# Four norm boundaries of a transformer kernel, taken in token halves

## The chip, the cores and the metric

The kernel runs on one core of a Trainium2 chip. The metric is device time in microseconds (us), the median of several executions; less is better. The engines are TensorE (PE in the profile; PEld are its weight loads), VectorE (DVE), ScalarE (ACT), GpSimd (POOL) and the SP queue, which issues the weight transfers. Each runs its own instructions in order; they wait for one another by semaphores.

## The reference

Two layers on 512 tokens (256 context, 256 latent) of width 1024, in float32. Each layer is a half-step SwiGLU FFN, a token mixer (layer 0: gated DeltaNet beside differential attention; layer 1: retention) and another half-step FFN. Every sub-layer reads a normalised and modulated input and is added back through a gate:

```python
def ada_in(x, g, m, s):
    return rms_norm(x, g) * (1 + m[:, 3 * s + 1][:, None, :]) + m[:, 3 * s][:, None, :]
def swiglu(h, w_in, w_out):
    g, u = jnp.split(h @ w_in, 2, axis=-1)
    return (jax.nn.silu(g) * u) @ w_out
...
        x = x + 0.5 * ada_gate(m_lat, 0) * swiglu(ada_in(x, norm_w[l, 0], m_lat, 0), ffn_w_in[l, 0], ffn_w_out[l, 0])
```

`rms_norm` divides each token by the root of its mean square over the 1024 features. Context tokens use their own modulation vector. The last norm is plain.

## The kernel before

**Layout.** `x` is held transposed: 8 chunks (`KD`) of 128 features on the partitions, 512 tokens along a row, context in columns 0 to 255 (`CTX`), latent in 256 to 511 (`LAT`). A float32 product is made of three products in `F32R`: weights and activations are each split in a hi and a lo part, and lo x hi, hi x lo and hi x hi are added in PSUM. Products on 512 columns are lines 812 to 814 (up and mixer steps, `products`) and 883 to 885 (`pe_down`). Where only latent tokens are live, `joint_products` (824, 825) runs w_hi on 512 columns, the hi and lo halves together, and w_lo on 256.

**Steps.** All weights go through one list of steps, `runs`. A step has a weight tile of up to 128x2048: SP loads `w_raw` (377), ScalarE copies it to `w_hi` (`split_hi`, 432), VectorE makes `w_lo` (`split_lo`, 586). There are two slots. The hi part of step s waits until step s-2's products are done, the load of step s until step s-2's lo part is made. TensorE starts step s when its lo part is there and its accumulator is free (`pe_ready`). Each engine's walk over a run of steps (`walk`) takes the first `skip` steps straight, then pairs in a hardware loop, then the rest.

**FFN.** The up steps make a gate and a value column block (16 x 3 products a step), ScalarE applies Silu (444; for latent alone a Copy at 441 and a Silu at 449), VectorE multiplies (620; 609 and 614), and the product is split (451, 625). The down steps (8 chunks, 12 or 10 blocks each, so 36 or 30 products) end in `x += gate * product` (653, two operations, one per stream). VectorE also works off `ada_tile`s (595), which make the modulation vectors from weights that GpSimd loads.

**A norm boundary.** While a down run whose sums are wanted goes on, ScalarE squares each new chunk of x (479) and VectorE adds the squares (644). After the last chunk, TensorE sums over partitions by products with ones (859), ScalarE takes the root (501), VectorE the reciprocal (699), TensorE broadcasts it to all partitions (899). Then, per chunk of 512 tokens, VectorE normalises (713), ScalarE scales and shifts, one operation per stream (513), ScalarE copies the hi part (518) and VectorE subtracts for the lo part (717). TensorE takes the first step of the next stage as the lo parts arrive. Seven norms: `n00` at the start, `n01` between the first FFN and the mixer (stage `diff`), `n02` after the mixer's output (`about`, 24 products a chunk) before `up1a`, `n10` before `up2a`, `n11` before retention (`retq`, latent columns alone, `joint_products`), `n12` and `fin`.

The order at a boundary is written out by hand, for VectorE as

```python
        dve_down(dve, "down0b", "n00", BOTH, 2, norm="n01")
        dve_mod(dve, "n01")
        dve_inverse(dve, "n01", 0)
        dve_modulate(dve, "n01")
        dve_left_tile(dve)
        dve_ab(dve)
```

In the retention queries ScalarE copies a step's result (1955), VectorE adds to it (2043), and TensorE rotates it (1885) after the next step's products.

Of the kernel before, what the change touches and what calls it, by code (L numbers as in the profile page):

```python
# [18 lines left out]
F32 = mybir.dt.float32  # L19
# [6 lines left out]
P = 128  # L26
D = 1024
# [98 lines left out]
def build(nc, a):  # L126
# [162 lines left out]
    def walk(eng, name, body, tallies=(), skip=0):  # L289
# [3 lines left out]
        looped = (n - 2 - skip) // 2  # L293
# [46 lines left out]
    chunks_before = {n: KD * i for i, n in enumerate(norms)}  # L340
# [93 lines left out]
    def act_up(act, name, cols):  # L434
# [18 lines left out]
        walk(act, name, body)  # L453
# [7 lines left out]
    def adds_before(norm):  # L461


        return 1 + (KD - 2) * (norms.index(norm) - 1)

    def sums_before(norm):

        return 0 if norm == "n00" else KD + norms.index(norm) - 1
# [15 lines left out]

    def act_down_norm(act, name, norm, cols):
        s0 = R[name][1]

        def body(s, slot, r, ahead):
            if isinstance(r, int) and r == KD - 1:

                act.activation(warm_root[:], vecs[:, 2:3], ACT.Sqrt).then_inc(warmed, 1)
# [4 lines left out]
        walk(act, name, body, skip=2)  # L496

# [37 lines left out]
    def scalar_program(act):  # L535
# [16 lines left out]
        act_root(act, "n01", 0, 1.0 / D)  # L552
        act_modulate(act, "n01")
        act_ab(act)
        act_down_norm(act, "about", "n02", ALL)
        act_root(act, "n02", 0, 1.0 / D)
        act_modulate(act, "n02")
# [4 lines left out]
        act_root(act, "n10", 0, 1.0 / D)  # L562
        act_modulate(act, "n10")
# [4 lines left out]
        act_root(act, "n11", 0, 1.0 / D)  # L568
        act_modulate(act, "n11")
# [63 lines left out]
    def dve_down(dve, name, norm_gate, streams, ada, norm=None):  # L633
# [6 lines left out]
        def body(s, slot, r, ahead):  # L640
            if norm and not (isinstance(r, int) and r < 2):
                dve.wait_ge(sq_ready, chunks_before[norm] + r)
# [3 lines left out]
            dve.wait_ge(step_done, s + 1)  # L646
# [12 lines left out]
            if ada and not (ada == 2 and isinstance(r, int) and r == KD - 1):  # L659
# [4 lines left out]
    def dve_left_tile(dve):  # L664
        ada_tile(dve, ada_next[0] - 1, (ada_next[0] - 1) % 2)
# [31 lines left out]
    def dve_inverse(dve, norm, t0):  # L697
        dve.wait_ge(root_done, norms.index(norm) + 1)
        dve.reciprocal(norm_columns(norm, t0, 8), norm_columns(norm, t0, 0)).then_inc(inverse_done, 1)

    def dve_modulate(dve, norm):

        base_c, cols = chunks_before[norm], streams_of(norm)
        dve.wait_ge(rstd_done, norms.index(norm) + 1)
# [28 lines left out]
    def vector_program(dve):  # L733
# [23 lines left out]
        dve_up(dve, "up0b", ALL, 2)  # L757
        dve_down(dve, "down0b", "n00", BOTH, 2, norm="n01")
        dve_mod(dve, "n01")
        dve_inverse(dve, "n01", 0)  # L760
        dve_modulate(dve, "n01")
        dve_left_tile(dve)
        dve_ab(dve)
        dve_gate(dve, "n01")
        dve_down(dve, "about", "n01", BOTH, 0, norm="n02")
        dve_mod(dve, "n02")
        dve_inverse(dve, "n02", 0)
        dve_modulate(dve, "n02")
# [1430 lines left out]
```

## Time and profile before

| | |
|---|---|
| median of three runs | 2210.33 us (2209.47 to 2213.39) |
| profiled execution | 2210.68 us, span 2209.0 us |
| TensorE busy | 2060.1 us, 93% of the span |
| VectorE busy | 1309.5 us, 59% |
| ScalarE busy | 794.9 us, 36% |
| mean granted TensorE clock | 0.966 |

Products are pipelined: a product's own time in the profile contains its way through the array, and what it costs in a row is the distance from one start to the next. The granted clock is 1.00 at 2.4 GHz and 0.50 at 1.2 GHz.

### The profile page before, as it was taken

How to read it: one execution, taken by the hardware profiler on the slowest of the kernel's cores; microseconds unless marked ns; L12 is line 12 of the kernel's file. 1: busy time of each engine (PE TensorE's matmuls, PEld its weight loads, DVE VectorE, ACT ScalarE, POOL GpSimd, SP SyncE). 2: the span in 40 equal slices, each digit the busy share in tenths (PEclk: the TensorE clock that was granted, in tenths of full speed). 3: DMA queues.
4: the chain of work that ended last, by engine and by line, in shares of the span. 5: the costliest groups of instructions: out<-in, count | busy, mean ns of one | idle time of the engine just before them, and what ended most of it. 6: DMA issues, size and time to landing. Idle time of an engine off the chain costs nothing.

```text
span 2209.0 us, 27575 instructions
## 1 busy us (share of the span) xinstructions
PE 2060.1 (93%) x9882; PEld 1721.1 (78%) x9882; DVE 1309.5 (59%) x1801; ACT 794.9 (36%) x1001; POOL 112.9 (5%) x173
## 2 busy tenths in 40 slices
PE   6999999897898978899999989999989999898998
PEld 6788888785587877788888878888877788677887
DVE  4677578746544675577677753363345524765666
ACT  2432222323444232532122253212234225846543
POOL 1000000000000230000000000000000000100000
PEclk9999999898898998999999999999998999999999
DMA  8355555521020000355555622343232223123453
GB/s 310 111 193 180 177 183 174 185 77 58 2 91 31 1 1 29 116 193 181 185 172 184 196 95 95 98 160 127 73 124 94 78 96 135 56 98 139 168 193 126
DMA packets 53989, 275.37 MB, mean 125 GB/s; under 512 B 6928, under 2 KB 8208, under 8 KB 36496
## 3 DMA queue, kind: packets, MB, share of 16 engines
q1 hardware_dynamic: 34032, 200.86, 26.5%
q0 software_dynamic: 19728, 72.88, 10.4%
q8 instruction: 58, 0.95, 0.2%
q10 hardware_dynamic: 144, 0.46, 0.1%
q14 instruction: 27, 0.22, 0.0%
HBM read 273.13 MB, written 1.05 MB: 124 GB/s over the span
## 4 chain that ended last, share of the span: by engine, by line
PE 81%; DVE 7%; ACT 6%; issue 4%; DMA 1%; ACTq 0%; DVEq 0%; POOL 0%; SPq 0%
PE ps L812 15%; PE ps L814 15%; PE ps L813 15%; PE ps L824 7%; PE ps L883 6%; PE ps L885 6%; PE ps L884 6%; PE ps L825 3%; ACT w_hi L432 1%; PE ps L921 1%; ACT sil L513 1%; DVE w_lo L586 1%; PE ps L1511 1%; PE ps L859 1%; PE ps L1507 1%
## 5 line engine op out<-in xcount | busy, mean ns | idle before, releaser
L812 PE MATMUL ps<-h_parts,w_lo 128*128 128x512 f32 x1480 | 585.5, 396 | 15.2 <-DVE h_parts L717 14.8
L813 PE MATMUL ps<-h_parts,w_hi 128*128 128x512 f32 x1480 | 580.8, 392 | 0.0
L814 PE MATMUL ps<-h_parts,w_hi 128*128 128x512 f32 x1480 | 580.4, 392 | 0.0
L432 ACT ACTIVATE w_hi<-w_raw 128x2048 fp32r<-128x2048 f32 (+3 forms) x207 | 354.0, 1710 | 532.7 <-PE ps L885 292.4
L586 DVE TENSOR_TENSOR w_lo<-w_raw,w_hi 128x2048 fp32r<-128x2048 f32 (+3 forms) x207 | 421.9, 2038 | 145.2 <-ACT w_hi L432 144.5
L595 DVE SCALAR_TENSOR_TENSOR ada_product<-ada_w,silu_c 128x1024 bf16<-128x1024 f32 x272 | 332.7, 1223 | 44.6 <-DMA ada_w<-in_ada 14.2
L812 PEld LDWEIGHTS ps<-h_parts,w_lo 128*128 128x128 f32 x1480 | 281.1, 190 | 78.1 <-issue 16.7
L813 PEld LDWEIGHTS ps<-h_parts,w_hi 128*128 128x128 f32 x1480 | 281.0, 190 | 59.4 <-issue 1.4
L814 PEld LDWEIGHTS ps<-h_parts,w_hi 128*128 128x128 f32 x1480 | 280.8, 190 | 59.4
L444 ACT ACTIVATE sil<-ps 128x512 f32<-128x512 f32 x66 | 39.5, 598 | 495.6 <-PE ps L814 495.6
L824 PE MATMUL ps<-h_parts,w_hi 128*128 128x512 f32 x544 | 200.4, 411 | 11.6 <-DVE h_parts L717 7.5
L883 PE MATMUL ps<-hid_parts,w_lo 128*128 128x512 f32 x528 | 205.4, 389 | 0.0
L884 PE MATMUL ps<-hid_parts,w_hi 128*128 128x512 f32 x528 | 205.4, 389 | 0.0
L885 PE MATMUL ps<-hid_parts,w_hi 128*128 128x512 f32 x528 | 205.4, 389 | 0.0
L620 DVE TENSOR_TENSOR prod<-sil,ps 128x512 f32<-128x512 f32 x66 | 45.4, 688 | 192.1 <-ACT sil L444 192.1
L825 PE MATMUL ps<-h_parts,w_lo 128*128 128x256 f32 x544 | 154.9, 285 | 0.0
L653 DVE SCALAR_TENSOR_TENSOR x<-ps,mod,x 128x256 f32 (+1 forms) x160 | 72.3, 481 | 132.0 <-PE ps L885 107.8
L824 PEld LDWEIGHTS ps<-h_parts,w_hi 128*128 128x128 f32 x544 | 104.6, 192 | 43.4 <-issue 6.9
L408 POOL DMA_DIRECT2D ada_w<-in_ada x136 | 72.0, 529 | 1038.5 <-DVE ada_product L595 1032.7
L884 PEld LDWEIGHTS ps<-hid_parts,w_hi 128*128 128x128 f32 x528 | 99.1, 188 | 20.7
L885 PEld LDWEIGHTS ps<-hid_parts,w_hi 128*128 128x128 f32 x528 | 99.1, 188 | 20.6
L883 PEld LDWEIGHTS ps<-hid_parts,w_lo 128*128 128x128 f32 x528 | 99.1, 188 | 20.5
(275 smaller groups left out, 2143.5 us busy)
## 6 DMA issues: line engine op xcount, KB each, us to landing
w_raw<-in_w_up SPq DMA_DIRECT2D x88, 1024.0 KB, 4.9
ada_w<-in_ada POOLq DMA_DIRECT2D x136, 512.0 KB, 3.8
w_raw<-in_w_down SPq DMA_DIRECT2D x32, 768.0 KB, 4.2
w_raw<-in_w_ret SPq DMA_DIRECT2D x24, 1024.0 KB, 4.9
w_raw<-in_w_down SPq DMA_DIRECT2D x32, 640.0 KB, 3.9
w_raw<-in_w_ab SPq DMA_DIRECT2D x14, 1024.0 KB, 4.9
w_raw<-in_w_ret_out SPq DMA_DIRECT2D x8, 1024.0 KB, 4.9
ada<-in_ada SPq DMA_DIRECT2D x8, 512.0 KB, 19.7
```

What stands on the lines that cost most here:

```text
L432: act.activation(w_hi[slot][:, 0:elems], w_raw[slot][:, 0:elems], ACT.Copy).then_inc(hi_ready, 1)
L586: dve.tensor_tensor(w_lo[slot][:, 0:elems], w_raw[slot][:, 0:elems], w_hi[slot][:, 0:elems].bitcast(F32), ALU.subtract).then_inc(lo_ready, 1)
L595: dve.scalar_tensor_tensor(out=ada_product[:], in0=ada_w[:, slot, :], scalar=1.0, in1=silu_c[:, st, :], op0=ALU.mult, op1=ALU.mult, accum_ ...
L653: last = dve.scalar_tensor_tensor(out=xc, in0=ps[:, 2 * slot, cols], scalar=mod[:, k, 2, st, bass.ds(r, 1)], in1=xc, op0=ALU.mult, op1=ALU ...
L812: pe.matmul(out, lo, rhs_hi(k), start=first and k == 0, stop=False)
L813: pe.matmul(out, hi, rhs_lo(k), start=False, stop=False)
L814: mm = pe.matmul(out, hi, rhs_hi(k), start=False, stop=last and k == nk - 1)
L824: pe.matmul(out, w_hi[slot][:, off:off + P], parts, start=start, stop=stop, skip_group_check=True)
L825: return pe.matmul(out[:, LAT], w_lo[slot][:, off:off + P], parts[:, 1], start=False, stop=stop, skip_group_check=True)
L883: pe.matmul(ps[:, 2 * slot, cols], wlo, hi, start=k == 0, stop=False)
L884: pe.matmul(ps[:, 2 * slot, cols], whi, lo, start=False, stop=False)
L885: mm = pe.matmul(ps[:, 2 * slot, cols], whi, hi, start=False, stop=k == nk - 1)
```

## The change

At `n01`, `n02`, `n10` and `n11` (`SEAMS`) the last two chunks of the down run and the first two steps of the next stage are taken in two halves of the tokens. The first half is CTX at the first three and LAT at `n11`.

- TensorE (`tail` in `pe_down`): chunk 6 and chunk 7 for the first half, each 3 x `nk` products of 256 columns; the first column sums of that half; chunk 6 for the second half, with the last two sums after its fourth block; the broadcasts of the first half; chunk 7 for the second half. Then `pe_seam_pairs`: step 0 and step 1 on the first half, then both on the second. Sums and broadcasts of the second half stand after the first, third and eighth block of step 0. At `n11`, `seam_queries` takes the two query steps whole (they have latent columns alone), with the same sums in between.
- VectorE (`dve_seam`): x updates by half. The modulation is three operations per chunk and half: VectorE `x * scale * broadcast`, ScalarE hi part `= scaled + shift`, VectorE lo part `= (scaled + shift) - hi`. Four scaled parts fit in `prod` and `sil`.
- The splits for the next stage's two steps stand inside this: the first before the first lo part, the second after the last lo part of the first half.
- `dve_mod` moves ahead of the down run. Two ada tiles instead of one are left for after the boundary (`n01`, `n10`).
- At `n11` ScalarE's first query copy and the first `retk` step wait for all lo parts.
- ScalarE's walk over the latent up runs (`up3a`, `up3b`) is straight code instead of a loop.

```diff
-    def walk(eng, name, body, tallies=(), skip=0):
+    def walk(eng, name, body, tallies=(), skip=0, unrolled=False):
...
-        looped = (n - 2 - skip) // 2
+        looped = 0 if unrolled else (n - 2 - skip) // 2
...
+    TAIL = KD - 2
+    SEAMS = {"n01": (CTX, LAT), "n02": (CTX, LAT), "n10": (CTX, LAT), "n11": (LAT, CTX)}
...
-        walk(act, name, body)
+        walk(act, name, body, unrolled=cols == LAT)
...
+    def act_seam(act, norm, s6):
...
+        act.activation(warm_root[:], vecs[:, 2:3], ACT.Sqrt).then_inc(warmed, 1)
+        for i in range(2):
+            act.wait_ge(sq_added, adds_before(norm) + TAIL - 2 + i)
+            square(0, i)
+        root(0)
+        split_hi(act, s6 + 2, s6 % 2, ELEMS[s6 + 2])
+        for c in range(4):
+            shift(0, c)
+        square(1, 0)
+        shift(0, 4)
+        shift(0, 5)
+        square(1, 1)
+        shift(0, 6)
+        shift(0, 7)
+        split_hi(act, s6 + 3, (s6 + 1) % 2, ELEMS[s6 + 3])
+        root(1)
+        for c in range(KD):
+            shift(1, c)
...
+    def dve_seam(dve, norm, gate, s6):
...
+        for i in range(2):
+            dve.wait_ge(seam_made, seam_count(norm, 0, 1) + i + 1)
+            place(0, i)
+        dve.wait_ge(mod_ready, k + 1)
+        inverse(0)
+        scale(0, 0)
+        scale(0, 1)
+        dve.wait_ge(step_done, s6 + 1)
+        place(1, 0)
+        scale(0, 2)
+        scale(0, 3)
+        split_lo(dve, s6 + 2, s6 % 2, ELEMS[s6 + 2])
+        for c in range(4):
+            low(0, c)
+            scale(0, c + 4)
+            if c == 0:
+                dve.wait_ge(step_done, s6 + 2)
+                place(1, 1)
+        for c in range(4, KD):
+            low(0, c)
+        split_lo(dve, s6 + 3, (s6 + 1) % 2, ELEMS[s6 + 3])
+        inverse(1)
...
+    def pe_seam_pairs(pe, name, norm, s6):
+        s0 = R[name][1]
+        for half, cols in enumerate(SEAMS[norm]):
+            for r in range(2):
+                slot = (s0 + r) % 2
+                if half == 0:
+                    pe_ready(pe, s0 + r)
+                for k in range(KD):
+                    if r == 0:
+                        pe.wait_ge(seam_lo, seam_count(norm, half, KD) + k + 1)
+                    for u in range(2):
+                        mm = products(pe, ps[:, 2 * slot + u, cols], slot, u * D + k * P, 1, lambda _: h_hi[:, k, cols],
+                                      lambda _: h_lo[:, k, cols], k == 0, k == KD - 1)
+                    if half == 0:
+                        pe_seam_second(pe, norm, s6, KD * r + k)
...
+        def tail(pe):
+            s6 = s0 + TAIL
+            for i in range(2):
+                pe_ready(pe, s6 + i)
+                half_chunk(i, 0).then_inc(seam_made, 1)
+            pe_seam_sum(pe, norm, 0, s6, 0)
...
+            half_chunk(0, 1, first).then_inc(step_done, 1)
+            pe_seam_spread(pe, norm, 0)
+            half_chunk(1, 1).then_inc(step_done, 1)
...
+            if r == 0:
+                act.wait_ge(seam_lo, seam_count("n11", 2, KD))
```

## Rows read from the trace of the kernel before

**Rows 1.** The page: busy time

```profile
PE 2060.1 (93%) x9882; PEld 1721.1 (78%) x9882; DVE 1309.5 (59%) x1801; ACT 794.9 (36%) x1001; POOL 112.9 (5%) x173
```

**Rows 2.** Stretches around the four boundaries; busy time by engine, granted clock

```profile
413.08:462.37 49.29, 43.36 (x181) 35.33 (x180) 31.41 (x45) 23.70 (x34) 1.58 (x3) 0.86 0.39 133
890.60:936.68 46.08, 39.30 (x169) 32.13 (x168) 29.29 (x44) 24.48 (x36) 0.60 (x1) 0.89 0.31 108
1260.36:1309.46 49.10, 42.58 (x182) 34.23 (x180) 31.76 (x48) 26.09 (x37) 1.58 (x3) 0.90 0.39 134
1633.14:1676.77 43.63, 35.35 (x151) 27.60 (x150) 23.77 (x33) 24.53 (x36) 0.00 (x0) 0.80 0.23 79
```

**Rows 3.** The same view of the hole between down run and mixer

```profile
426.68:437.53 10.85, 5.16 (x26) 4.56 (x25) 6.45 (x14) 5.40 (x9) 0.53 (x1) 0.61 0.61 225
```

**Rows 4.** Timeline of the first boundary

```profile
413.08 0.39 PE L883 MATMUL ps<-hid_parts,w_lo 128*128 128x512 f32 x1
...
426.45 0.39 PE L885 MATMUL ps<-hid_parts,w_hi 128*128 128x512 f32 x1
...
429.42 1.87 PE L859 MATMUL ps<-const,prod 128*128 128x1 f32 x8 [0.92 <-ACT prod L479]
...
431.92 2.07 PE L899 MATMUL ps<-const,small 128*128 128x128 f32 x8 [0.64 <-DVE small L699]
...
437.53 0.76 PE L812 MATMUL ps<-h_parts,w_lo 128*128 128x512 f32 x1 [3.53 <-DVE h_parts L717]
```

**Rows 5.** The stretch after that hole

```profile
437.53:442.65 5.12, 5.12 (x12) 4.05 (x13) 3.54 (x6) 4.72 (x9) 0.00 (x0) 0.50 0.00 0
```

**Rows 6.** Groups of instructions by form; mean ns of one

```profile
L586 DVE TENSOR_TENSOR w_lo<-w_raw,w_hi 128x2048 fp32r<-128x2048 f32 x134 | 306.9, 2291 | 119.8 <-ACT w_hi L432 119.7
L812 PEld LDWEIGHTS ps<-h_parts,w_lo 128*128 128x128 f32 x1480 | 281.1, 190 | 78.1 <-issue 16.7 <-DVE h_parts L717 2.9 <-ACT df_o L1095 0.7
...
L432 ACT ACTIVATE w_hi<-w_raw 128x2048 fp32r<-128x2048 f32 x134 | 256.1, 1911 | 260.9 <-PE ps L814 153.5 <-PE ps L885 68.7 <-PE ps L825 26.3
...
L513 ACT ACTIVATE sil<-prod,mod 128x256 f32<-128x256 f32 x88 | 48.3, 591 | 37.9 <-DVE prod L713 37.4
...
L653 DVE SCALAR_TENSOR_TENSOR x<-ps,mod,x 128x256 f32 x96 | 43.3, 481 | 88.0 <-PE ps L885 73.8 <-PE ps L825 13.3 <-DVE mod L689 0.4
...
L614 DVE TENSOR_TENSOR prod<-sil 128x256 f32<-128x256 f32 x22 | 9.2, 418 | 0.0
...
L451 ACT ACTIVATE hid_parts<-prod 128x256 f32 x18 | 7.5, 418 | 37.8 <-DVE prod L614 37.8
...
L449 ACT ACT_TABLE_LOAD x5 | 6.4, 1283 | 0.1
```

**Rows 7.** Timeline of one latent up step with table load

```profile
2040.69 0.50 PE L824 MATMUL ps<-h_parts,w_hi 128*128 128x512 f32 x1 [1.06 <-DVE w_lo L586]
```

**Rows 8.** Stretches in the two latent up runs and one wait in the queries

```profile
2014.46:2075.10 60.64, 57.21 (x322) 48.83 (x321) 37.19 (x41) 41.51 (x50) 0.00 (x0) 1.00 0.47 165
2121.74:2161.29 39.55, 39.55 (x226) 34.27 (x225) 26.11 (x29) 21.84 (x28) 0.00 (x0) 1.00 0.51 176
...
1690.20:1691.40 1.20, 0.00 (x0) 0.00 (x0) 0.69 (x1) 1.20 (x2) 0.00 (x0) 1.00 1.00 423
```

**Rows 9.** Timeline of latent products, 512 and 256 columns in turn

```profile
2100.00 0.40 PE L824 MATMUL ps<-hid_parts,w_hi 128*128 128x512 f32 x1
...
2100.23 0.28 PE L825 MATMUL ps<-hid_parts,w_lo 128*128 128x256 f32 x1
...
2100.35 0.39 PE L824 MATMUL ps<-hid_parts,w_hi 128*128 128x512 f32 x1
```

**Rows 10.** Timeline of VectorE ahead of the third boundary

```profile
1260.79 0.88 DVE L653 SCALAR_TENSOR_TENSOR x<-ps,mod,x 128x256 f32 x2 [1.03 <-PE ps L885]
...
1263.29 1.22 DVE L595 SCALAR_TENSOR_TENSOR ada_product<-ada_w,silu_c 128x1024 bf16<-128x1024 f32 x1
...
1264.67 1.23 DVE L595 SCALAR_TENSOR_TENSOR ada_product<-ada_w,silu_c 128x1024 bf16<-128x1024 f32 x1 [0.16 <-DVE ada_product L595]
```

More of the change, by code:

```diff
@@ L339, in build, with seam_count, stream, token_tiles @@
     norms = ["n00", "n01", "n02", "n10", "n11", "n12", "fin"]
-    chunks_before = {n: KD * i for i, n in enumerate(norms)}
+    TAIL = KD - 2
+    SEAMS = {"n01": (CTX, LAT), "n02": (CTX, LAT), "n10": (CTX, LAT), "n11": (LAT, CTX)}
+    whole = [n for n in norms if n not in SEAMS]
+    chunks_before = {n: KD * i for i, n in enumerate(whole)}
+    seam_before = {n: i for i, n in enumerate(SEAMS)}
+    squares_before, count = {}, 0
+    for n in norms:
+        squares_before[n] = count
+        count += TAIL if n in SEAMS else KD
+    seam_made, seam_placed, seam_squared = sem("seam_made"), sem("seam_placed"), sem("seam_squared")
+    seam_summed, seam_rooted, seam_inverse, seam_spread = (sem(f"seam_{n}") for n in ("summed", "rooted", "inverse", "spread"))
+    seam_scaled, seam_hi, seam_lo = sem("seam_scaled"), sem("seam_hi"), sem("seam_lo")
+    def seam_count(norm, half, per):
+        return (2 * seam_before[norm] + half) * per
+    def stream(cols):
+        return 0 if cols == CTX else 1
+    def token_tiles(cols):
+        return range(cols.start // P, cols.stop // P)
     ups_before = {}
@@ L496, in act_down_norm, with scaled_part, square, root @@
         walk(act, name, body, skip=2)
+    def scaled_part(c, cols):
+        return (prod[:, 0, cols], prod[:, 1, cols], sil[:, 1, cols], sil[:, 0, cols])[c % 4]
+    def act_seam(act, norm, s6):
+        k = norms.index(norm)
+        done = seam_count(norm, 0, 1)
+        def square(half, i):
+            cols = SEAMS[norm][half]
+            if half == 0:
+                act.wait_ge(seam_placed, done + i + 1)
+            else:
+                act.wait_ge(acc_free, s6 + i + 3)
+            act.activation(prod[:, (s6 + i) % 2, cols], x[:, TAIL + i, cols], ACT.Square).then_inc(seam_squared, 1)
+        def root(half):
+            t = token_tiles(SEAMS[norm][half])
+            act.wait_ge(seam_summed, done + half + 1)
+            act.activation(norm_columns(norm, 0, 0)[:, t.start:t.stop], ps[:, SEAM[half], t.start:t.stop], ACT.Sqrt,
+                           bias=vecs[:, 2:3], scale=1.0 / D).then_inc(seam_rooted, 1)
+        def shift(half, c):
+            cols = SEAMS[norm][half]
+            act.wait_ge(seam_scaled, seam_count(norm, half, KD) + c + 1)
+            act.activation(h_hi[:, c, cols], scaled_part(c, cols), ACT.Identity,
+                           bias=mod[:, k, 1, stream(cols), c:c + 1]).then_inc(seam_hi, 1)
+        act.activation(warm_root[:], vecs[:, 2:3], ACT.Sqrt).then_inc(warmed, 1)
[16 more added lines that the diff above has]
+            shift(1, c)
     def act_root(act, norm, t0, scale):
@@ L658, in body @@
                 split_lo(dve, s + 2, slot, ahead)
-            if ada and not (ada == 2 and isinstance(r, int) and r == KD - 1):
+            if ada:
                 ada_tile(dve, t0 + r, (t0 + slot + R[name][1]) % 2)
@@ L861, in pe_ssq, with pe_seam_sum @@
         return mm
+    def pe_seam_sum(pe, norm, half, s6, part):
+        cols, bank = SEAMS[norm][half], SEAM[half]
+        if part == 0:
+            pe.wait_ge(sq_added, adds_before(norm) + TAIL - 1)
+        pe.wait_ge(seam_squared, 4 * seam_before[norm] + 2 * half + part + 1)
+        operands = (sil[:, 0], prod[:, s6 % 2]) if part == 0 else (prod[:, (s6 + 1) % 2],)
+        for n, squares in enumerate(operands):
+            for t in token_tiles(cols):
+                mm = pe.matmul(ps[:, bank, t:t + 1], squares[:, t * P:(t + 1) * P], ones[:, 0:1],
+                               start=part == 0 and n == 0 and t == cols.start // P, stop=part == 1, skip_group_check=True)
+        if part == 1:
+            mm.then_inc(seam_summed, 1)
```

170 lines of the change are left out of this document (129 added, 41 removed).

## The prediction

> **What bounds the kernel now.** Start with the page. TensorE is busy 93% of the span [rows 1], so time can only be saved where TensorE stands or runs slowly. The stretches around the four boundaries show where. I take each from the first product of the second-last down chunk (t = 0 below) to the first product of the third step after the boundary: 49.29, 46.08, 49.10 and 43.63 us, at a mean granted clock of 0.80 to 0.90 [rows 2]. At the first, 10.85 us lie between the last down product and the first product of the next stage [rows 3]. The timeline shows what fills them: 1.0 us of waiting and the column sums (429.42), the broadcasts (431.92), then TensorE waits 3.53 us more for VectorE's first lo part and starts at 437.53 [rows 4]. ScalarE's and VectorE's splits for the next two steps run in the same hole. The clock falls in it and stays at 0.50 for the first twelve products, which take 5.12 us [rows 5], 0.427 each; sixty before the hole, the first at 413.08 and the last at 426.45 [rows 4], are 0.227 apart, so the low clock costs 12 x 0.2 = 2.4 us. Over the whole stretch this boundary loses 49.3 - 156 x 0.227 = 13.9 us (sixty down products, 96 of two steps); the second loses 46.1 - 144 x 0.227 = 13.4 and the third 13.7.
>
> A second place is the last up loop. In the first of its two runs table loads of 1.28 us stand between ScalarE's copy and Silu (five are recorded at 449) [rows 6], the split is late by them, and TensorE waits for lo weights, 1.06 us at 2040.69 [rows 7]. Ten such steps take 60.64 us, while seven steps without loads take 39.55 us, 5.65 us each [rows 8].
>
> **Prices.** A 256-column product: 2100.23 to 2100.35, 0.117 us, with its own weights and with the next ones loaded meanwhile; a 512-column one takes 0.23 beside it [rows 9]. This is the number on which the change hangs, because it makes 1032 half products (456 in the chunk pairs, 576 in the steps) out of 516 whole ones: 1032 x 0.117 - 516 x 0.227 = 3.6 us. Lower bound: half of 0.227, which is nothing extra. Upper bound: the 0.19 us that one weight load is shown with [rows 6], which would be 79 us extra. I take 0.117, since that row is the very form.
>
> VectorE, 256 columns: 0.481 us with PSUM, 0.418 without; two in a row take 0.88 [rows 10], so 0.40 apart. I take 0.44 for a scale or an x update and 0.46 for a lo part, which the next scale waits for. ScalarE: 0.418 plain, 0.591 with scale and bias [rows 6]; the new shift has a bias only, I take 0.50 with the handover. Splits: 1.91 and 2.29 us for 2048 elements [rows 6], the latter 2.25 when work follows. Column sums and broadcasts: eight take 1.87 and 2.07 us at the low clock [rows 4], 0.23 and 0.26 each; bounds are that and half of it, and I take half, 0.11, as the clock should be high.
>
> The Trainium skill speaks against half products: "TensorE: Matmul & The Clock Gate", What overlaps and what doesn't, says that a weight load overlaps running products only when its row group differs. All loads here use all rows. With that page's formula the load is about 107 ns, so the half products would come to some 0.213 us and the change would be about 99 us dearer than by the row, as an estimate. The row does not agree: 768 columns and two loads take 0.35 us together [rows 9].
>
> **First boundary, step by step** (us after t = 0). Half chunks of 30 products take 3.5. TensorE: 3.5, 7.0 (both chunks, first half), four sums 7.45, twelve products 8.85, two sums 9.1, eighteen 11.2, two broadcasts 11.4, last half chunk 14.9. The first needs of this are met: the second chunk's lo weights are there at 2.9 as before (VectorE goes on from that split at 1263.29, t being 1260.36) [rows 10]; x update, square and add for the first half end near 8.2, before the second sums; root and reciprocal near 9.9, before the broadcasts. An ada tile of 2.6 us (two operations 1.38 apart [rows 10]) stands ahead of the first x update on VectorE and still leaves it at 6.3.
>
> From the broadcasts on VectorE is the path: handover 0.16, four scales and an x update 2.2, split of the next step's weights 2.25 (its hi part, asked for at 11.4, is done by 13.3), lo part 0.46, handover 0.15: 5.2. First product 16.6, so TensorE stands 1.7. VectorE then offers a lo part every 0.92, the second after 1.38 (another x update), while TensorE needs 0.70; the fourth scale of the second four ends 3.7 after the first lo part. ScalarE's shift (0.55) and split of the following weights (1.96), VectorE's split (2.25), reciprocal (0.2) and the broadcasts (0.4) follow: second step's first half starts 8.9 after the first, at 25.5. In it TensorE has 5.6 + 0.7 of work, so 2.6 stay empty. From there on nothing is missing: first half 5.6, two second halves 11.2; VectorE finishes the second half's lo parts at 32.4, the first is wanted at 31. End 42.3 against 49.3: **7.0 saved**.
>
> The third step's weights must be ready by then. Step one now ends at 36.7 only, 5.6 before step two. ScalarE's split 38.9; VectorE has two left ada tiles instead of one: four operations 1.38 apart [rows 10], 5.4, from 32.4 to 37.8; copy of step one 1.22 (the width of the tile's operation), split 2.25: 41.5 with the handovers. Covered by 0.8; without that cover the surplus is paid one for one. The SP queue's load of the third step waits for the first split (16.1) and has 20 us. Moving the modulation vectors ahead of the down loop (three operations on 16 columns) costs nothing: all its ada tiles precede it, and VectorE stands 1 us per chunk there [rows 10].
>
> **Other boundaries.** The third is the same: 49.1 - 42.3 = **6.8**; after it the gate and the up product take the copy's place, still under 42.3. The second has chunks of 24 products: broadcasts end at 9.3, first product 14.5, end 40.2: 46.1 - 40.2 = **5.9**; TensorE stands 2.4 there first, as only 2.8 of the 5.2 is covered. At the fourth only the chunks are halved; the two query steps take latent columns and run whole. Here the change adds a wait: ScalarE's copy of the first query step waits for all sixteen lo parts (32.4), since it overwrites scaled parts. Behind it stand its split and, on TensorE, the rotation. Copy and split to 34.9, VectorE's split 37.2: third step at 37.4 where it was 43.6, **6.2**. TensorE is through with step two at 31 and stands 6.
>
> **Up loop.** Ten steps at 5.65 are 56.5 for 60.64: **4.1**, if no load is left; the second up loop of this stage shows the same instructions without one [rows 8]. "ScalarE: Activation LUTs", Table sets, in the Trainium skill has copy in every set; that fits.
>
> Sum 7.0 + 5.9 + 6.8 + 6.2 + 4.1 = 30.0. The profiled execution took 2210.68 (span 2209.0), 0.35 above the median of 2210.33: **2180.3 us**. Most of each hole is not removed, it is cut into two pauses with work between.
>
> **Rivals.** (1) *The pauses are longer and the clock falls in them.* Fourteen VectorE operations and four handovers stand on the path: 0.05 to 0.1 more each is 1 us a boundary. For a fall: a mean of 0.61 over the 10.85 us at the first boundary [rows 3] means that it came after (0.61 - 0.5) / 0.5 x 10.85 = 2.4 us, with sums running. Against: a wait of 1.3 us at 1690 passed at 1.00 [rows 8]. A fall costs up to 2.4; 3.4 x 4 = 13.6 less: 2194. The 1.7 us of slack in the second pause hides part. (2) *Half products are bound by their weight loads.* The slower side: 1032 x (0.19 - 0.117) = 75, so 2180 + 75 = 2255. It turns the sign when a half product takes 0.117 + 30/1032 = 0.146. Against it stands the form's own row. (The page on TensorE named above states a rule of this kind.) (3) *The boundary does not shrink*: the same splits and 256-column operations with twice the fixed part refill the hole; only the up loop's 4.1 stays, 2206. For it: the new path holds two VectorE splits and one of ScalarE, 6.5 us, where the old hole held one of each, 4.2. Against: 3.5 us of down products and 5.6 of the first step now lie beside it. (4) *More gain*: VectorE at 0.40 throughout and no third pause at the queries, 2172.
>
> **Chances.** Forecast 0.55, (1) 0.23, (2) 0.07, (3) 0.06, (4) 0.06, something slower that I do not see 0.03. Around 2180 the unknown prices (0.40 to 0.48 on VectorE, 0.42 to 0.59 on ScalarE) move it by 5 either way. The range that leaves out no more than two in ten reaches from 2172 to 2198. Of a measurement here 0.2%, 4.4 us, can be told from nothing. Faster by more: the forecast, (1), (4) and 0.01 of (3), 0.85; within: the rest of (3), 0.05; slower: 0.10.
>
> **What would show it.** Half products spaced 0.117 to 0.12; pauses of about 1.7 and 2.6 us (2.4 and 2.6 at the second, one of 6 in the queries) in place of 10.7; granted clock 1.00 from t = 0 to 42; the ada tiles after the second lo parts, with no TensorE wait behind them; no table loads in the last up steps. Wrong if the spacing is 0.15 or more, if VectorE's chain from broadcast to lo part is over 7 us, or if the third step waits for its split.

## The result and the profile after

The changed kernel takes 2190.44 us in the median of six runs (2185.98 to 2194.33), the kernel before 2210.68 beside it: ratio 0.991, 95% interval 0.9897 to 0.9922. That is 20 us less, inside the range (2172 to 2198); 30 less were forecast. The profiled execution took 2188.84 us (span 2187.2), 21.8 less than the one of before. The page's first line, to be held against [rows 1]:

```profile
PE 2058.6 (94%) x10430; PEld 1748.2 (80%) x10430; DVE 1319.4 (60%) x1865; ACT 761.3 (35%) x972; POOL 112.9 (5%) x173
```

The four boundaries, cut at the same two products as in [rows 2]; after start, end and length come the busy time of TensorE's products, its weight loads, VectorE, ScalarE and GpSimd, then the granted clock, the DMA share and GB/s:

```profile
413.24:457.32 44.08, 42.84 (x345) 42.58 (x344) 33.52 (x58) 18.15 (x29) 1.58 (x3) 0.96 0.36 126
884.16:927.51 43.35, 41.39 (x322) 41.22 (x320) 26.72 (x50) 19.05 (x31) 0.00 (x0) 0.92 0.24 88
1251.22:1294.97 43.75, 41.51 (x345) 41.12 (x344) 33.93 (x61) 20.56 (x32) 1.58 (x3) 1.00 0.37 125
1618.68:1657.19 38.51, 32.28 (x220) 29.26 (x218) 25.99 (x47) 21.04 (x32) 0.00 (x0) 0.92 0.26 89
```

They save 5.2, 2.7, 5.35 and 5.1 us, 18.4 together, where 7.0, 5.9, 6.8 and 6.2 were forecast, 25.9. TensorE's timeline at the first boundary, and the second pause at the third:

```profile
413.24 0.28 PE L1060 MATMUL ps<-hid_parts,w_lo 128*128 128x256 f32 x1
413.36 0.28 PE L1061 MATMUL ps<-hid_parts,w_hi 128*128 128x256 f32 x1
...
420.50 0.58 PE L1010 MATMUL ps<-const,sil 128*128 128x1 f32 x4
420.94 0.58 PE L1010 MATMUL ps<-const,prod 128*128 128x1 f32 x4
421.38 0.36 PE L1060 MATMUL ps<-hid_parts,w_lo 128*128 128x256 f32 x1
...
425.50 0.60 PE L1019 MATMUL ps<-const,small 128*128 128x128 f32 x4
425.86 0.36 PE L1060 MATMUL ps<-hid_parts,w_lo 128*128 128x256 f32 x1
...
429.41 0.28 PE L1062 MATMUL ps<-hid_parts,w_hi 128*128 128x256 f32 x1
430.93 0.35 PE L947 MATMUL ps<-h_parts,w_lo 128*128 128x256 f32 x1 [1.24 <-DVE h_parts L776]
...
439.61 0.60 PE L1019 MATMUL ps<-const,small 128*128 128x128 f32 x4
...
1275.88 0.28 PE L949 MATMUL ps<-h_parts,w_hi 128*128 128x256 f32 x1
1277.15 0.71 PE L1019 MATMUL ps<-const,small 128*128 128x128 f32 x4 [1.00 <-DVE small L756]
```

Pauses are given here from the start of one product to the start of the next; 0.12 of that is the spacing that two products always have. The hole of 10.85 us [rows 3] is now one pause of 1.52 at the first boundary, ahead of the first product of the next stage, and two at the third, 1.52 and 1.27. At the first boundary the second pause is missing in this trace: TensorE ran at the low clock before it and was late itself. From the first half product to the end of chunk 7's last are 16.3 us where 14.9 were forecast. At the second boundary the first pause is longer and the clock falls behind it:

```profile
897.31 0.28 PE L1062 MATMUL ps<-h_parts,w_hi 128*128 128x256 f32 x1
899.55 0.35 PE L947 MATMUL ps<-h_parts,w_lo 128*128 128x256 f32 x1 [1.96 <-DVE h_parts L776]
```

The stretches at the low clock behind the first pause of the first two boundaries, with the busy times of the instructions on `h_parts` alone (no GpSimd column):

```profile
432.80:436.20 3.40, 2.89 (x14) 2.67 (x14) 2.35 (x6) 1.37 (x3) 0.50 0.58 243
900.40:907.20 6.80, 4.96 (x22) 4.71 (x22) 2.93 (x7) 1.59 (x4) 0.50 0.36 143
```

VectorE and ScalarE behind the first broadcasts of the first boundary:

```profile
425.75 1.92 ACT L456 ACTIVATE w_hi<-w_raw 128x2048 fp32r<-128x2048 f32 x1 [2.05 <-PE ps L1062]
...
428.10 2.29 DVE L654 TENSOR_TENSOR w_lo<-w_raw,w_hi 128x2048 fp32r<-128x2048 f32 x1
430.31 0.48 DVE L776 SCALAR_TENSOR_TENSOR h_parts<-prod,mod,h_parts 128x256 fp32r<-128x256 f32 x1
...
434.88 1.90 ACT L456 ACTIVATE w_hi<-w_raw 128x2048 fp32r<-128x2048 f32 x1
436.68 0.24 ACT L546 ACTIVATE small<-ps,vecs 128x2 f32<-128x2 f32 x1
...
436.81 2.29 DVE L654 TENSOR_TENSOR w_lo<-w_raw,w_hi 128x2048 fp32r<-128x2048 f32 x1 [0.79 <-ACT w_hi L456]
439.02 0.16 DVE L756 RECIPROCAL small<-small 128x2 f32<-128x2 f32 x1
```

Ten steps of the first latent up run (60.64 in [rows 8]):

```profile
1995.10:2051.65 56.55, 56.55 (x322) 49.05 (x321) 37.43 (x40) 32.62 (x43) 0.00 (x0) 1.00 0.47 164
```

At the Copy and the Silu of these steps the kernel before has ten table loads recorded, five at each line (441 and 449); the changed one has one, in both runs together. The third steps behind the first three boundaries start without a wait, as forecast.

The whole account of the two profiled executions: boundaries 18.4 less, first up run 4.1 less, second 1.0 less, the mixer behind the first boundary 1.4 less; the retention stage, from the third step after the fourth boundary to the last norm's sums, is 3.3 longer (320.0 against 316.7). That makes 21.6 of 21.8.

### The profile page after: what moved, and what is told of

Read it like the earlier page. It is cut to its first block, busy times and chain, and to the rows that moved or that the text cites. A ratio compares the mean times of both kernels' runs of the same rounds, so it can differ in the third digit from the quotient of the medians.

```text
span 2187.2 us, 28339 instructions
## 1 busy us (share of the span) xinstructions
PE 2058.6 (94%) x10430; PEld 1748.2 (80%) x10430; DVE 1319.4 (60%) x1865; ACT 761.3 (35%) x972; POOL 112.9 (5%) x173
## 4 chain that ended last, share of the span: by engine, by line
PE 85%; DVE 7%; ACT 4%; issue 2%; DMA 1%; POOL 0%; SPq 0%; ACTq 0%; DVEq 0%
PE ps L947 15%; PE ps L948 15%; PE ps L949 15%; PE ps L959 8%; PE ps L1100 5%; PE ps L1101 5%; PE ps L1102 5%; PE ps L960 4%; PE ps L1138 1%; DVE w_lo L654 1%; ACT w_hi L456 1%; PE ps L1724 1%; PE ps L1720 1%; DMA const<-in_const 1%; PE ps L1060 1%
## 5 line engine op out<-in xcount | busy, mean ns | idle before, releaser
L947 PE MATMUL ps<-h_parts,w_lo 128*128 128x512 f32 (+1 forms) x1576 | 601.2, 381 | 8.4 <-DVE h_parts L776 4.4
L948 PE MATMUL ps<-h_parts,w_hi 128*128 128x512 f32 (+1 forms) x1576 | 596.7, 379 | 0.0
L949 PE MATMUL ps<-h_parts,w_hi 128*128 128x512 f32 (+1 forms) x1576 | 596.3, 378 | 0.0
L947 PEld LDWEIGHTS ps<-h_parts,w_lo 128*128 128x128 f32 x1576 | 299.8, 190 | 65.1 <-issue 5.3
L948 PEld LDWEIGHTS ps<-h_parts,w_hi 128*128 128x128 f32 x1576 | 299.6, 190 | 55.4 <-issue 1.4
L949 PEld LDWEIGHTS ps<-h_parts,w_hi 128*128 128x128 f32 x1576 | 299.5, 190 | 54.5
L959 PE MATMUL ps<-h_parts,w_hi 128*128 128x512 f32 x544 | 198.1, 407 | 6.3 <-DVE h_parts L860 2.5
L1100 PE MATMUL ps<-hid_parts,w_lo 128*128 128x512 f32 x468 | 182.1, 389 | 0.0
L1101 PE MATMUL ps<-hid_parts,w_hi 128*128 128x512 f32 x468 | 182.1, 389 | 0.0
L1102 PE MATMUL ps<-hid_parts,w_hi 128*128 128x512 f32 x468 | 182.1, 389 | 0.0
L726 DVE SCALAR_TENSOR_TENSOR x<-ps,mod,x 128x256 f32 (+1 forms) x144 | 65.3, 481 | 121.1 <-PE ps L1102 96.9
L959 PEld LDWEIGHTS ps<-h_parts,w_hi 128*128 128x128 f32 x544 | 105.1, 193 | 33.9 <-DVE w_lo L654 5.0
L960 PEld LDWEIGHTS ps<-h_parts,w_lo 128*128 128x128 f32 x544 | 105.7, 194 | 0.2 <-issue 0.2
L1100 PEld LDWEIGHTS ps<-hid_parts,w_lo 128*128 128x128 f32 x468 | 87.8, 188 | 18.4
L1101 PEld LDWEIGHTS ps<-hid_parts,w_hi 128*128 128x128 f32 x468 | 87.8, 188 | 18.2
```

The lines of the kernel that those rows point to most:

```text
L947: pe.matmul(out, lo, rhs_hi(k), start=first and k == 0, stop=False)
L948: pe.matmul(out, hi, rhs_lo(k), start=False, stop=False)
L949: mm = pe.matmul(out, hi, rhs_hi(k), start=False, stop=last and k == nk - 1)
L959: pe.matmul(out, w_hi[slot][:, off:off + P], parts, start=start, stop=stop, skip_group_check=True)
L960: return pe.matmul(out[:, LAT], w_lo[slot][:, off:off + P], parts[:, 1], start=False, stop=stop, skip_group_check=True)
L1100: pe.matmul(ps[:, 2 * slot, cols], wlo, hi, start=k == 0, stop=False)
```

## The experiments

Each was run beside the kernel before; differences between kernels of one group are the better guide, since the same changed kernel gave 0.991 and 0.9896.

**The parts apart.** First the halves without the new order (`halves_only`): as many half products, in the old sequence.

```diff
+    def halved_pairs(pe, s, slot, norm=None):
+        for part in (CTX, LAT):
+            for k in range(KD):
+                ...
+                for u in range(2):
+                    mm = products(pe, ps[:, 2 * slot + u, part], slot, u * D + k * P, 1, ...)
```

> The kernel before with nothing changed but the width of products: the last two chunks of the four down runs and the first two steps after three of the boundaries (not after the fourth) are taken as 256-column products, all of the context half, then all of the latent half. No order between engines changes. 1032 half products in place of 516 whole ones, 96 x 3 = 288 of them in first steps that wait for lo parts anyway. Theory A (a product has a fixed part of about 0.014 us beside its columns, as 0.227 - 512 / 2400 columns per ns shows): half products are 0.1205 apart as in the changed kernel, so + 7.3 us at most, + 5 to 7 expected, 2216. Theory B (the row of the latent products, 0.117): + 3.6 at most, 2213. Rival C (bound by weight loads, 0.19): + 50 or more.

2235.46 us, ratio 1.0124 (1.0105 to 1.0143): slower by 26 us. The spacing settles what was asked: 120 half products stand 0.120 apart, which makes 7 us of the 26 (1032 x 0.120 against 516 x 0.227).

```profile
427.19 0.28 PE L894 MATMUL ps<-hid_parts,w_lo 128*128 128x256 f32 x1
427.31 0.28 PE L895 MATMUL ps<-hid_parts,w_hi 128*128 128x256 f32 x1
427.44 0.28 PE L896 MATMUL ps<-hid_parts,w_hi 128*128 128x256 f32 x1
```

The rest I had overlooked. The old modulation still takes both halves at once and gives a lo part only every 1.3 to 1.9 us. The first half of step 0 is paced by it to the end, and all of the second half comes behind:

```profile
437.56 0.69 DVE L717 TENSOR_TENSOR h_parts<-sil,h_parts 128x512 f32 x1 [1.37 <-ACT h_parts L518]
...
450.12 0.69 DVE L717 TENSOR_TENSOR h_parts<-sil,h_parts 128x512 fp32r<-128x512 f32 x1 [1.19 <-ACT h_parts L518]
```

This boundary took 55.80 us (413.16 to 468.96) for 49.29, at about the mean clock of before (0.88 for 0.86). The second took 53.60 for 46.08 and the third 57.39 for 49.10, and there the clock has a share as well: at the second it stayed at 0.50 for 20 us (before, 10), and the mean fell from 0.89 to 0.81:

```profile
894.99:948.59 53.60, 46.00 (x313) 43.59 (x312) 29.30 (x44) 24.47 (x36) 0.92 (x2) 0.81 0.28 100
```

No run parts the pacing from the clock. Halving alone costs; here it paid only together with a new order around it.

Then the straight loop alone (`unroll_only`):

```diff
-        looped = (n - 2 - skip) // 2
+        looped = 0 if unrolled else (n - 2 - skip) // 2
```

> The kernel before with ScalarE's latent up runs as straight code and nothing else. The prediction's term is 4.1 us, 2206.6. By the traces the change gave 4.1 in the first of the two runs (ten steps 60.6 to 56.5) and 1.0 in the second (nine steps 50.9 to 49.9), so 5.1, 2205.6, if both come from the straight code. If the second run's 1.0 comes from something else, 2206.6.

2205.68 us, ratio 0.9989 (0.9979 to 0.9998), 3.7 less, with an interval that reaches from 0.4 to 4.6. The trace is the better guide: the ten steps take 56.52 us for 60.64, 4.1 less.

```profile
2009.70:2066.22 56.52, 56.52 (x322) 48.98 (x321) 37.40 (x40) 32.60 (x42) 0.00 (x0) 1.00 0.48 164
```

And the boundaries without the straight loop (`seams_only`):

```diff
-        walk(act, name, body, unrolled=cols == LAT)
+        walk(act, name, body)
```

> The changed kernel with ScalarE's latent up runs in a loop again; the boundaries stay in halves. If the terms add up it gives 20.2 - 5.1 = 15 us against the kernel before, 2195.5; the four stretches around the boundaries measured 18.4 together in the two traces, the rest of the mixers' stages takes some back. A rival, that part of what the boundaries seem to give is only shifted into the later stages, would show as less than 12.

2193.55 us, ratio 0.9936 (0.9917 to 0.9956), 15.9 less. 15.9 and 3.7 add up to 19.6, within noise of the 20.2 measured together, and the shortfall lies in the part with the boundaries (25.9 forecast).

**The two pauses.** Four kernels in one group. First the changed kernel once more (`after_again`):

> The changed kernel itself, once more, as the measure for the three kernels beside it. Its first six runs spread over 8 us, so its place against the kernel before is taken again: 2190 us, ratio 0.991.

2187.9 us, 0.9896 (0.988 to 0.9912). Its first boundary took 43.81 with the clock at 1.00 where it took 44.08 with a fall: there a fall costs only 0.3, because the second pause (1.27) takes it up. The four together took 169.5 us, for 169.7.

Then `early_split`: ScalarE rounds the following weights before its fifth shift (not the first, as the expectation has it), and VectorE takes the reciprocal before it splits them.

```diff
         square(1, 0)
+        split_hi(act, s6 + 3, (s6 + 1) % 2, ELEMS[s6 + 3])
         shift(0, 4)
...
-        split_lo(dve, s6 + 3, (s6 + 1) % 2, ELEMS[s6 + 3])
         inverse(1)
+        split_lo(dve, s6 + 3, (s6 + 1) % 2, ELEMS[s6 + 3])
```

> At the first boundary of the changed kernel ScalarE makes the first half's shifted chunks before it rounds the next weights (w_hi, 1.9 us), and VectorE splits those weights (2.3 us) before it takes the reciprocal for the second half. Here the rounding stands ahead of the first shift and the split behind the reciprocal. Theory 1, the second pause ends with VectorE's chain reciprocal, scale, place, so what stands in front of it counts: the pause at the second half shrinks by 0.8 to 1.1 us in each boundary, 3 to 4 us in all, 2186 to 2187 us. Theory 2, the weights split is what the second half's last products wait for or the first pause grows by the rounding's 1.9 us as the shifts come later: no gain or up to 4 us slower. The pause ahead of the first product after the half chunks tells them apart: 1.5 us stays (theory 1) or grows (theory 2).

2184.56 us, 0.9878 (0.9861 to 0.9895). The runs of the two kernels overlap in time; in the trace the second pause is gone, and the boundaries take 42.55, 43.33, 42.49 and 36.94 us, 4.4 less than the first trace of the changed kernel and 4.1 less than the second. 1.3 of it is the first boundary and 1.3 the third, both at a clock of 1.00 before and after. Theory 1; the first pause stayed 1.52.

```profile
436.12 0.16 DVE L756 RECIPROCAL small<-small 128x2 f32<-128x2 f32 x1
436.19 2.27 DVE L654 TENSOR_TENSOR w_lo<-w_raw,w_hi 128x2048 fp32r<-128x2048 f32 x1
```

```profile
438.15 0.28 PE L949 MATMUL ps<-h_parts,w_hi 128*128 128x256 f32 x1
438.27 0.60 PE L1019 MATMUL ps<-const,small 128*128 128x128 f32 x4
```

Then `filled`, the changed kernel with products in its pauses that nobody reads:

```diff
+    def fill(pe, count):
+        for _ in range(count):
+            pe.matmul(ps[:, 7, 0:SEQ], ident, const[:, C_COSD:C_COSD + SEQ], start=True, stop=True)
...
+            fill(pe, 5)
...
+            fill(pe, 6 if nk == FB else 9)
```

The five stand ahead of the second half's broadcasts, the six or nine behind the last half chunk.

> The changed kernel with TensorE products that nobody reads put into its two pauses at each boundary (6 or 9 of 256 columns in fp32 behind the last half chunk, 5 ahead of the second half's broadcasts). It computes the same. Theory 1, the pauses cost twice, once as idle time and once by the clock of 1.2 GHz that follows them (3.4 us after the first pause at the first boundary, 6.8 us at the second): with the pauses filled the granted clock stays at 1.00 in the boundaries, and the time falls by 1.7 us at the second boundary and 0.3 to 0.6 at the others, 2 to 3 us in all, 2187 to 2188 us. Theory 2, the clock falls for what went before the pauses (the spaced sums and broadcasts) and not for them: the clock falls as before, and the time stays or grows by what the fillers take beyond the pauses, up to 1 us for each boundary.

2193.73 us, 0.9928 (0.9914 to 0.9943): slower than the changed kernel, and still theory 1 on the clock. It stayed at 1.00 through the first three boundaries, of which two are shown:

```profile
413.28:459.11 45.83, 45.83 (x368) 45.17 (x366) 33.51 (x58) 18.15 (x29) 1.58 (x3) 1.00 0.35 122
887.34:931.43 44.09, 44.09 (x349) 43.36 (x348) 26.71 (x50) 18.94 (x31) 0.00 (x0) 1.00 0.24 86
```

But I had sized a filler at 0.24 us. In fp32 the trace records each as two rows, 0.216 apart, so six take 2.6 us in a pause of 1.5 and hold up the product behind them:

```profile
429.56 2.75 PE L1044 MATMUL ps<-const 128*128 128x256 f32 x12
431.97 0.47 PE L947 MATMUL ps<-h_parts,w_lo 128*128 128x256 f32 x1
```

`both` has the edits of early_split and of filled.

> The two edits together. If both theories 1 hold and don't overlap: 5 to 7 us below the changed kernel, 2183 to 2185 us. If the shorter second pause already keeps the clock up, the gains don't add: 3 to 5 us.

2198.14 us, 0.9948 (0.9934 to 0.9962). Neither expectation: with five fillers in the second pause the fillers are what the broadcasts wait for, and moving the split can't help (first boundary 45.83 again).

**What sets the first pause.** Three kernels on top of early_split. `split_first`:

```diff
         place(1, 0)
+        split_lo(dve, s6 + 2, s6 % 2, ELEMS[s6 + 2])
         scale(0, 2)
         scale(0, 3)
-        split_lo(dve, s6 + 2, s6 % 2, ELEMS[s6 + 2])
```

> early_split, and VectorE splits the next weights (2.29 us) straight behind the placing, before the third and fourth scaling and not after them. Theory 1, the first pause is the ring of weights: the slot comes free with the first whole-chunk half (425.4 us at the first boundary), then ScalarE's rounding 1.92, VectorE's split 2.29 and one low operation 0.48 follow, against 4.0 us of half products, so the split's start counts, and it was held by two scalings until 428.10 where the rounding had ended at 427.67: the pause falls from 1.52 to 1.1 us (from 2.24 to 1.8 at the second boundary), 0.4 each, 1.6 us in all below early_split. Theory 2, VectorE's whole queue up to the last low operation sets the pace and not the split's place in it: the 0.4 us come back as small waits between the first half's products, and the time equals early_split's.

2191.16 us, 0.9915 (0.9901 to 0.9928). Both theories missed: the pause grew, from 1.52 to 1.90.

```profile
427.74 2.29 DVE L654 TENSOR_TENSOR w_lo<-w_raw,w_hi 128x2048 fp32r<-128x2048 f32 x1 [0.30 <-ACT w_hi L456]
429.94 0.87 DVE L769 SCALAR_TENSOR_TENSOR sil<-x,mod,ps 128x256 f32<-128x256 f32 x2
430.73 0.48 DVE L776 SCALAR_TENSOR_TENSOR h_parts<-prod,mod,h_parts 128x256 fp32r<-128x256 f32 x1
```

The two scalings still stand ahead of the first lo part, and VectorE now idles 0.30 for ScalarE's rounding. The first product waits for the sum of VectorE's queue, not for the split's place in it. The four boundaries together took 3.8 us more than in early_split (169.1 for 165.3), and the ratio is 0.0037 higher, 8 us; the longer pause is 1.5 of that, the rest is not explained.

`split_parts`:

```diff
+        def split_part(n):
+            ...
+            part = [w[s6 % 2][:, 0:2 * D].rearrange("p (u d) -> p u d", u=2)[:, :, n * D // 2:(n + 1) * D // 2]
+                    for w in (w_lo, w_raw, w_hi)]
+            dve.tensor_tensor(part[0], part[1], part[2].bitcast(F32), ALU.subtract) \
+               .then_inc(lo_ready if n else seam_split, 1)
```

> early_split, and the split of the next weights in two operations, chunks 0 to 3 before the first low operation and chunks 4 to 7 before the fourth; TensorE waits for the second at its fifth chunk. Theory 1 (the ring of weights): the pause falls by half a split, 1.1 us, to 0.4 us (1.1 at the second boundary), and the fifth chunk may wait 0.5 us: 2.5 to 4.4 us below early_split. Theory 2 (VectorE's whole queue sets the pace): the fifth chunk waits for all that the pause gave back, and the time equals early_split's.

2187.92 us, 0.9893 (0.9878 to 0.9908). Theory 2 at the first boundary: the pause fell to 0.45, the fourth chunk then came 0.81 behind the sums ahead of it and the fifth 0.31 behind the fourth, and the boundary took 42.54 for 42.55. The second took 40.73 for 43.33: its pause was 1.17 for 2.24, and the low clock behind it lasted 3.4 us for 6.8, so that this gain is in good part the clock's. At the fourth boundary, whose products are written out apart and wait for the whole split, my edit made them wait for its later second half, 4.2 us:

```profile
1633.65 0.28 PE L1078 MATMUL ps<-hid_parts,w_hi 128*128 128x256 f32 x1
1637.88 0.80 PE L970 MATMUL ps<-h_parts,w_hi 128*128 128x512 f32 x1 [3.95 <-DVE w_lo L786]
```

The fillers once more, shorter and in the first pause only (`fit`; the diff is against both):

```diff
-            fill(pe, 5)
...
-            fill(pe, 6 if nk == FB else 9)
+            fill(pe, 3 if nk == FB else 4)
```

> early_split with unread fp32 products only in the first pause, and by the length that the filled kernel showed of one (two rows of 0.216 us): 3 of them, 1.3 us in a pause of 1.52, and 4, 1.7 us in 2.24 at the second boundary. In the filled kernel the granted clock stayed at 1.00 in the first three boundaries, but its fillers were longer than the pauses and held the path. Theory 1, the clock falls for the pause: it stays at 1.00 at the second boundary, whose 43.33 us become 41.6 to 42, and nothing else is late; 1.5 to 3 us below early_split. Theory 2, what the rest of the pause leaves idle is enough to let the clock fall: as early_split.

2183.65 us, 0.9881 (0.9865 to 0.9897): as early_split in the median (which had 0.9878). So the times don't tell the theories apart. In the trace the second boundary is where theory 1 has it, and below: 40.26 for 43.33, at 1.00, with the first at 42.55 as in early_split.

```profile
413.50:456.05 42.55, 42.55 (x351) 42.05 (x350) 33.40 (x58) 18.16 (x29) 1.58 (x3) 1.00 0.40 132
883.36:923.62 40.26, 40.03 (x330) 39.50 (x329) 26.61 (x50) 18.92 (x31) 0.00 (x0) 1.00 0.26 95
```

Last, the split in two operations again, at the first three boundaries only, with fillers where a pause stays (`parts_fit`; the diff is against split_parts and fit):

```diff
         for c in range(4):
-            if c == 3:
-                split_part(1)
             low(0, c)
+            if c == 3 and norm != "n11":
+                split_part(1)
             scale(0, c + 4)
...
-            fill(pe, 3 if nk == FB else 4)
+            fill(pe, {"n02": 2, "n11": 3}.get(norm, 0))
```

> fit, with the split in two operations at the first three boundaries only (the fourth has its products written out elsewhere, where TensorE still waits for the whole split), and its second operation behind the fourth low operation and not ahead of it. The fillers stay where a pause of over 1 us stays: 2 at the second boundary, 3 at the fourth. Theory 1, the place of the split counts: the pause is 0.45 us, and the fifth chunk, which split_parts served 1.0 us late, is served 0.4 to 0.5 us late, so the boundaries take 42.0 us (42.55 in fit) and 39.8 (40.26): 1.5 us in all below fit, ratio 0.9875. Theory 2, VectorE's queue up to the last low operation sets the pace: the boundaries take what they took in fit, within 0.1 us. That would be too little for the medians, so the boundaries' own times in the trace decide.

2178.39 us (2177.78 to 2183.63), ratio 0.9859 (0.9842 to 0.9875): the fastest here, 32 us below the kernel before, though its profiled execution, the slowest of its runs, has a span of 2182.0 where fit's has 2179.9. The boundaries took 42.39, 40.12, 42.34 and 36.96 us, 0.15 less than in fit at each of the first three: nearer theory 2. That is 0.5 us in all four for 5 in the medians, and the intervals of the two ratios overlap (fit's is 0.9865 to 0.9897), so this pair doesn't show that parts_fit is the faster. The first pause gave 1.07 back, the fifth chunk took 0.78:

```profile
433.96 0.28 PE L963 MATMUL ps<-h_parts,w_hi 128*128 128x256 f32 x1
434.87 0.35 PE L961 MATMUL ps<-h_parts,w_lo 128*128 128x256 f32 x1 [0.62 <-DVE h_parts L777]
```

**The floor under smaller products.** `quarter` cuts the half products of the two last down chunks once more:

```diff
-                pe.matmul(ps[:, 2 * slot + half, cols], wlo, hi, start=k == 0, stop=False)
+                for t in range(2):
+                    pe.matmul(ps[:, 2 * slot + half, tile], wlo, hi[:, q], start=k == 0, stop=False, ...)
```

> The changed kernel with each half product of the two last down chunks cut once more, into two of 128 columns with the same weights loaded for each (240 for 120 at a boundary of ten chunks, 192 for 96 at the second). It computes the same. Theory 1, a product costs its columns and a fixed 0.014 us (512 columns 0.227, 256 columns 0.120): 0.067 us apart, 1.6 us more for each boundary, 6 us in all. Theory 2, the load of 128 rows of weights is a floor that 256 columns only just cover: the column sums, a weight load each with one column, stand 0.084 to 0.110 apart, and the quarter products do too: 6 to 12 us more for each boundary, 22 to 45 in all.

One run, 2285.83 us. Against the expectation, the sums of these two chunks aren't the reference's; why was not tested. Only the times are read.

```profile
413.29 0.28 PE L1063 MATMUL ps<-hid_parts,w_hi 128*128 128x128 f32 x1
413.40 0.28 PE L1064 MATMUL ps<-hid_parts,w_hi 128*128 128x128 f32 x1
413.52 0.28 PE L1062 MATMUL ps<-hid_parts,w_lo 128*128 128x128 f32 x1
```

```profile
413.23:428.30 15.07, 15.07 (x137) 15.06 (x135) 6.31 (x10) 4.11 (x6) 0.53 (x1) 1.00 0.43 154
428.30:453.90 25.60, 25.60 (x123) 25.60 (x122) 5.29 (x9) 4.59 (x8) 0.00 (x0) 0.50 0.11 42
```

Theory 2: 120 such products stand 0.111 apart, hardly closer than half products of twice the columns at 0.120. 912 of them in place of 456 are 46 us, theory 2's upper figure; the time is 95 us above the changed kernel's, for a reason in neither theory: the granted clock fell to 0.50 although TensorE was never idle (15.07 busy of 15.07), and stayed there for 34 us. By the mean clocks of the two traces (0.947 and 0.971) some 115 us more ran at the low level, which is worth up to 57 us, as an estimate.

## Why the prediction was right, and where it was off

**Half products.** Right in kind, a little mis-sized: 0.120 apart and not 0.117. Over 1032 products that is 3.1 us more, 6.7 in all for halving. 0.117 was read from one pair whose neighbour was a 512-column product; for halves among themselves the longer row is the price. Rival 2 (0.19 us each) is excluded. Its bound was a recorded duration; quarter shows that products with a load each can stand 0.111 apart while each load is still recorded with 0.19. By the rule in the Trainium skill, "TensorE: Matmul & The Clock Gate", What overlaps and what doesn't, the halves would have stood near 0.213, as the prediction estimated; the measurement decides against it. The same page of the Trainium skill, LDWEIGHTS, gives the time of a load as its columns divided by 1.2 ns, an estimate of 107 ns for 128; the 0.111 of quarter agrees with that.

**Column sums and broadcasts.** The largest term that was mis-sized, and by a misreading. The eight of [rows 4] that take 1.87 us are four instructions, one for every 128 tokens, since each fp32 product is recorded as two, like the fillers. I took 0.11 us, half of what one record takes at the low clock, for a whole instruction. At full clock four sums hold TensorE 0.88 us (420.50 to 421.38), not 0.45. In the first boundary of early_split, at 1.00 with a single pause, 42.55 us less 312 half products at 0.120 and less 1.4 for the pause leave 3.7 us for 16 sums and broadcasts, 0.23 each with the later start of the product behind them; the forecast's steps have 1.6. That is 2.1 more a boundary, 6.3 at the first three.

**The pauses** (here without the spacing of 0.12). First: forecast 1.7, measured 1.4; the chain from the end of the broadcasts to the first product takes 5.1 us (425.86 to 430.93) for 5.2, while the last half chunk takes TensorE longer. Second: forecast 2.6, measured 1.15 at the third boundary, since TensorE had more of its own to do in the same 8.8 us. At the second boundary it is absent (broadcasts 0.12 behind the products), and at the first in the trace with a fall. So the chain through VectorE and ScalarE, on which the forecast rests, was priced well. That the pauses came out shorter is the other side of the dearer TensorE work: early_split, without a second pause, still needs 42.5 where 42.3 was the forecast with two.

**The clock.** Forecast 1.00 throughout. In the trace shown it fell at three of the four boundaries, so rival 1's mechanism came, though not its 13.6 us. It held at the third boundary and in one of two traces at the first. At the second it fell in all six traces that had no filler there (for 6.8 us, or 3.4 in split_parts, whose pause is 1.17) and in none of the four that had one, and fit shows the price by filling the idle time alone: 3.1 us, for a boundary of 40.26. That the pause brings it about there is shown by these four. That 40.26 is the 40.2 of the forecast is luck: the dearer sums and the missing second pause cancel. The queries' wait of 1.3 us at 1.00, which I set against a fall, was shorter than this pause of 2.24. But length alone doesn't order the cases: behind a pause of 1.52 the clock fell in 5 of 12 cases (changed kernel twice, seams_only and early_split, at the first, third and fourth boundary), behind one of 1.9 in 1 of 3. What else counts was not found.

**The fourth boundary.** Forecast 37.4 and a stand of 6 us in the queries; measured 38.5, with gaps of 3.23 and 2.77 around the rotation. The clock fell twice, for 3.4 us behind the first pause and for 6.8 in those gaps. early_split brings it to 36.9, and there the first of the two falls is absent; how much of the 1.6 is the clock and how much the order, no run shows.

**Up loop.** 4.1 forecast, 4.1 measured in the trace, with the table loads gone; alone 4.1 in its trace and 3.7 by the medians. The 1.0 in the second run does not come from the straight loop, which without the boundaries left its steps at 5.65. Straight steps run at either 5.55 or 5.65 us for a whole run of ten, in either up run, the same code (fit has 5.55 in the first run and 5.65 in the second, the changed kernel the reverse). What chooses was not found.

**Sum.** Forecast 30.0, measured 20.2 by the medians. Of the 7.5 us missed at the boundaries, 6.4 are at the first three. There the sums cost 6.3 more and the half products 2.7 (912 x 0.003), the clock costs 1.7 at the first and 3.1 at the second, together 13.8; the pauses, 13.6 in the forecast and 6.1 measured, give 7.5 back. So it was partly luck that the range held: a misread price on TensorE and the falls of the clock were made up for by half, because they ran into idle time that the forecast had left. Behind the fourth boundary 3.3 us are lost again. early_split, fit and parts_fit show a like stretch (336.8 to 338.0 us from that third step to ScalarE's second split of the first latent up run, 334.6 before), so it is not chance; its cause stays open. Rivals 3 and 4 did not come, and of rival 1 the falls came but not the longer pauses.

## What to carry to other kernels

Cutting an operation in two to overlap a hole costs before it pays: halves_only lost 26 us and the full reorder won 16 with as many half products; in the one the modulation still came in whole chunks, in the other every producer went by halves. Price a cut by the spacing of a row of such pieces among themselves, not by a recorded duration (0.19 against 0.111) nor by one pair of unlike neighbours, and see how many records one instruction leaves before taking a price from them. When the hole has become small pauses, look at the queue of the engine that feeds it: an operation that nobody awaits yet, put behind one that somebody does, took the second pause away; moving work about within what is all awaited moved the wait by 0.78 of 1.07 us to the next chunk.

## What the runs showed of the hardware

- Products with a weight load each, of 128, 256 and 512 columns, stand 0.111, 0.120 and 0.227 us apart at full clock, 0.214, 0.213 and 0.427 at half clock. Cutting below 256 columns gains next to nothing.
- The granted clock fell behind a first pause of 2.24 us or more in all five traces with one, behind one of 1.17 in the one trace that had it at the second boundary, behind 1.52 in 5 of 12 cases, and not at the second boundary where unread products filled the pause until 0.61 or 0.41 us (start to start) before the next product. It also fell in quarter, with TensorE busy throughout (15.07 of 15.07 us) on products of 128 columns.
- An fp32 product of 256 columns takes 0.43 us and is recorded as two, 0.216 apart; a column sum or broadcast in fp32 leaves two records too and takes some 0.22. The kernel's own products, in the rounded form, take 0.120.
